# The table of relative biases: 128 copies written to DRAM and read back reversed, in place of matmuls that reverse it

## The reference, cut to what matters

```python
def block(args):
    i, qi = args
    qpos = i * Q_BLOCK + jnp.arange(Q_BLOCK)      # Q_BLOCK = 128
    rel = qpos[:, None] - kpos[None, :]
    bias = bias_table[t5_bucket(rel)].transpose(2, 0, 1).astype(jnp.float32)
    logits = jnp.einsum('bhmqd,bhmkd->bhmqk', qi, kt).astype(jnp.float32) * scale
    logits = logits + bias[None, :, None]
    logits = jnp.where(rel >= 0, logits, -1e30)
```

## Time and profile before

| | us |
|---|---|
| median of three runs | 2764.8 (2764.6 to 2765.83) |
| the profiled execution | 2764.3 |
| its span, first to last instruction | 2762.5 |
| TensorE busy | 2686.8 |
| DVE busy | 1798.8 |
| ACT busy | 1323.2 |
| GpSimd busy | 247.5 |

### The profile page before, as it was taken

How to read it: one execution, slowest core, us unless ns; L and a number is a source line. 1 busy time by engine, 2 the same in 40 slices (tenths; PEclk the granted TensorE clock), 3 DMA queues, 4 the chain that set the end, 5 groups by cost and what they waited for, 6 DMA issues and landing times.

```text
span 2762.5 us, 47112 instructions
## 1 busy us (share of the span) xinstructions
PE 2686.8 (97%) x18110; PEld 2474.7 (90%) x18110; DVE 1798.8 (65%) x2093; ACT 1323.2 (48%) x1603; POOL 247.5 (9%) x181
## 2 busy tenths in 40 slices
PE   8999999999999999999999999799799999999997
PEld 8999899889999888888888889799788888889996
DVE  6676456555545677777764467996677777775444
ACT  4543364464434555555543344544355555554332
POOL 4001200001101100000001231601200000000100
PEclk9999999999999999999999999899899999999998
DMA  7545455545435565555555555355355566555552
GB/s 244 187 157 183 139 182 168 168 165 192 163 122 171 175 189 189 189 189 187 188 189 184 189 185 179 115 177 182 117 179 185 189 189 189 189 189 183 179 186 103
DMA packets 189152, 485.28 MB, mean 176 GB/s; under 512 B 15021, under 2 KB 15029, under 8 KB 188752
## 3 DMA queue, kind: packets, MB, share of 16 engines
q1 hardware_dynamic: 187216, 474.02, 52.8%
q0 software_dynamic: 1792, 9.17, 0.9%
HBM read 481.02 MB, written 2.11 MB: 175 GB/s over the span
## 4 chain that ended last, share of the span: by engine, by line
PE 91%; DVE 6%; ACT 1%; issue 1%; DMA 0%; SPq 0%; ACTq 0%; POOL 0%; DVEq 0%
PE ps L1736 91%; DVE w_lo L1075 2%; DVE op L1121 1%; DVE acc L1550 1%; ACT w_hi L661 1%; DVE hbuf L1706 1%; DVE x_res L1709 0%; DMA raw<-in_weights 0%; ACT op L696 0%; SPq L508 0%; ACT hbuf L1048 0%; ACT yres L1040 0%; ACT L686 0%; DVE mq L1093 0%; DVE rstd L1105 0%
## 5 line engine op out<-in xcount | busy, mean ns | idle before, releaser
L1736 PE MATMUL ps<-op,w_hi 128*128 128x256 f32 (+1 forms) x7232 | 1699.4, 329 | 48.0 <-DVE op L1121 28.5
L1075 DVE TENSOR_TENSOR w_lo<-raw,w_hi 128x1024 fp32r<-128x1024 f32 x900 | 1124.7, 1253 | 866.0 <-ACT w_hi L661 865.1
L661 ACT ACTIVATE w_hi<-raw 128x1024 fp32r<-128x1024 f32 x900 | 950.3, 1059 | 1165.1 <-PE ps L1736 1148.7
L1736 PE MATMUL ps<-op,w_lo 128*128 128x256 f32 x5024 | 1182.8, 281 | 0.0
L1736 PEld LDWEIGHTS ps<-op,w_hi 128*128 128x128 f32 x7232 | 1126.5, 192 | 55.0 <-issue 32.8
L1736 PEld LDWEIGHTS ps<-op,w_lo 128*128 128x128 f32 x5024 | 957.9, 191 | 125.8
L1736 PE MATMUL ps<-g,w_hi 128*128 128x256 f32 (+1 forms) x2112 | 474.8, 319 | 0.0
L1736 PE MATMUL ps<-g,w_lo 128*128 128x256 f32 x1408 | 340.0, 282 | 0.0
L1736 PEld LDWEIGHTS ps<-g,w_hi 128*128 128x128 f32 x2112 | 326.1, 188 | 0.0
L1736 PEld LDWEIGHTS ps<-g,w_lo 128*128 128x128 f32 x1408 | 264.3, 188 | 32.4
L1736 PE MATMUL ps<-w_hi,op 128*128 128x512 f32 x512 | 163.5, 394 | 0.0
(11 more groups left out here) (257 smaller groups left out, 1534.1 us busy)
## 6 DMA issues: line engine op xcount, KB each, us to landing
raw<-in_weights SPq DMA_DIRECT2D x900, 512.0 KB, 4.2
x_res<-in_x SPq DMA_DIRECT2D x8, 256.0 KB, 7.6
mem_x<-in_mem POOLq DMA_DIRECT2D x1, 2048.0 KB, 8.6
x_res<-in_x POOLq DMA_DIRECT2D x1, 2048.0 KB, 9.8
out_x<-x_res POOLq DMA_DIRECT2D x8, 256.0 KB, 2.3
rel_rev<-rel_dram POOLq DMA_DIRECT2D x1, 1024.0 KB, 6.0
hg_con<-in_hg_consts POOLq DMA_DIRECT2D x1, 576.0 KB, 7.4
par<-in_params POOLq DMA_DIRECT2D x1, 538.0 KB, 7.0
```

What stands on the lines that cost most here:

```text
L661: nc.scalar.activation(w_hi[:, s], raw[:, s], ACT.Copy).then_inc(hi_rounded, 1)
L1075: TT(w_lo[:, s], raw[:, s], w_hi[:, s].bitcast(F32), ALU.subtract).then_inc(chunk_split, 1)
L1736: return nc.tensor.matmul(out, lhsT, rhs, start=start, stop=stop, skip_group_check=True)
```

## The change

The rows are written to DRAM 128 times instead of once: `rel_dram` grows to 128 x 8 x 384, and the source repeats `rel_row` with a step of zero. The load then reads, for partition p, copy p from element 127 - p on (a step of one copy less one element), and writes into `bias` itself. The reversal matmuls, their matrix `flip` and its load, ACT's four copies and the waits between them go. TensorE waits for `std_ready` before block 1 instead of at chunk 14, and DVE waits for `rel_loaded` before its first softmax.

```diff
-            pool.dma_start(flip[:, :], A["flip"]).then_inc(table_loaded, 16)
@@ x_and_table, GpSimd
                 if j == 4:
                     pool.wait_ge(rel_copied, 1)
-                    pool.dma_start(rel_dram, rel_row[:, :]).then_inc(rel_stored, 16)
+                    pool.dma_start(rel_dram.rearrange("p h n -> h p n"), spread(rel_row[:, :], P)).then_inc(rel_stored, 16)
                 if j == 6:
                     pool.wait_ge(rel_stored, 16)
-                    shifted = bass.AP(rel_dram.tensor, 0, [[1, P], [NREL, HEADS], [1, TOK]])
-                    pool.dma_start(rel_rev[:, :, :], shifted).then_inc(rel_loaded, 16)
+                    shifted = bass.AP(rel_dram.tensor, P - 1, [[HEADS * NREL - 1, P], [NREL, HEADS], [1, TOK]])
+                    pool.dma_start(bias[:, :, :], shifted).then_inc(rel_loaded, 16)
@@ ACT
-            def bias_out():
-
-                for j in range(4):
-                    act.wait_ge(bias_flipped, j + 1)
-                    nc.scalar.activation(bias[:, 2 * j:2 * j + 2], results(1, j), ACT.Copy).then_inc(bias_made, 1)
-
@@ softmax_top, DVE
                 if item == 0:
-                    dve.wait_ge(bias_made, 4)
+                    dve.wait_ge(rel_loaded, 16)
@@ beside_first, TensorE
                 if (b, c) == (0, 5):
-                    pe.wait_ge(table_loaded, 48)
+                    pe.wait_ge(table_loaded, 32)
                     mm(ps[0:HEADS, 4, 0:NREL], relb[0:33, :], onehot[:, :], True, True).then_inc(rel_sum, 1)
                 if (b, c) == (0, 12):
                     pe.wait_ge(consts_loaded, 32)
                     sums(0, True)
-                if (b, c) == (0, 14):
-                    pe.wait_ge(rel_loaded, 16)
+                if (b, c) == (1, 0):
                     pe.wait_ge(std_ready, STD_END[0])
-                    for h in range(HEADS):
-                        last = mm(ps[:, 4 + h // 2, (h % 2) * TOK:(h % 2 + 1) * TOK], flip[:, :], rel_rev[:, h], True, True)
-                        if h % 2:
-                            last.then_inc(bias_flipped, 1)
-                if (b, c) == (1, 0):
-                    pe.wait_ge(bias_made, 4)
```

More of the change, by code:

```diff
@@ L258, in build @@
         bias = slab("bias", 80)
-        rel_rev = slab("rel_rev", 40)
         rel_row = inside("rel_row", [HEADS, NREL], 72 * KB)
         onehot = inside("onehot", [33, NREL], 74 * KB)
-        flip = inside("flip", [P, P], 77 * KB)
         lam_in = inside("lam_in", [P, 4, 64], 76 * KB)
@@ L308, in build @@
         ps = ctx.enter_context(nc.psum_tensor("ps", [P, 8, BANK], F32))
-        rel_dram = nc.dram_tensor("rel_dram", [HEADS, NREL], F32, kind="Internal").ap()
+        rel_dram = nc.dram_tensor("rel_dram", [P, HEADS, NREL], F32, kind="Internal").ap()
         def pc(name, i=0, n=1):
@@ L333, in build @@
         dve_steps, act_steps = sem("dve_steps"), sem("act_steps")
-        rel_sum, rel_copied, bias_flipped, bias_made = (sem(n) for n in ("rel_sum", "rel_copied", "bias_flipped", "bias_made"))
+        rel_sum, rel_copied = sem("rel_sum"), sem("rel_copied")
         lam_summed, lam_exped, lb_shifted, lb_exped = (sem(n) for n in ("lam_summed", "lam_exped", "lb_shifted", "lb_exped"))
@@ L745, in _ @@
             run_product(act, GM["hg_fm"], split, nothing, both(by_slot(in_pair, SLOTS, range(2, 8)), at_slot(11, exponents),
-                                                               at_slot(15, in_root), at_slot(17, bias_out)), also=beside_f)
+                                                               at_slot(15, in_root)), also=beside_f)
             def level_exps(level):
```

## The result

| | median, us | runs | against before (95% interval) |
|---|---|---|---|
| before | 2765.3 | 4 | |
| after | 2795.6 (2792.1 to 2797.1) | 4 | 1.0104 (1.0092 to 1.0117) |

The account below looks back on a forecast made before the run. TensorE, busy 97% of the span, was taken as the bound. Later sums +25.2, removed matmuls -3.3 and lower clock +2.3 gave +24.2 us on 2764.3, 2788.5, stated as 2789 us; range 2770 to 2800 us.

Parts of the forecast that it names:

- What bounds the kernel, and the place to watch: TensorE, 97% busy; at chunk 12 its sumsq matmuls wait for GpSimd's last sum, ready just 0.07 us before.
- What goes: Reversal matmuls on TensorE's path: -3.26 us; ACT's copies, the load of flip and the moved waits: nothing.
- The store: GpSimd's wait for rel_stored: 8 source partitions set the rate, 31 us plus 2.7, landing at 67.8 us; chance 0.64.
- The fixed part: Part of the store's issue-to-landing time that comes on top of the transfer: 2.9 - 0.2 = 2.7 us.
- The eight-engine rival: Store on eight engines at their own speed: 13.6 + 2.7 = 16.3 us, time 2771 to 2772; chance 0.15.
- GpSimd's tail: After the store lands, GpSimd issues the load and sums two pairs: 5.9 us, sums ready at 73.7 us.
- The clock: After TensorE's idle time before the sumsq matmuls, 4.64 us at half speed: +2.3 us.
- The larger transfer also crosses the weight loads: nothing: At 34 to 45 us only two or three weight loads in flight, TensorE stands before needing later ones: no cost.
- the quick store: At GpSimd's wait: store over 16 engines lands after 9.5 us, time 2762 to 2764.5; chance 0.18.

Follow-up runs that it names:

- the kernel without copies: Changed kernel, but its store writes one 12 KB copy and the load steps by one element, leaving the reversal out: 2761.2 us, ratio 0.9986.
- step 4: Changed kernel with the store's eight source rows on partitions 0, 4, ... 28 instead of 0 to 7: 2775.2 us in one run.
- the kernel with the late load: Changed kernel with the load of bias, and the wait for the store before it, moved behind the load of hg_con: 2775.2 us, ratio 1.0036.

## Why the prediction was right, point by point

*What bounds the kernel, and the place to watch*: right. The sums before chunk 12 had no cover, and the shift appears there.

*What goes*: right. -3.26 us were forecast, -4.3 measured with 3.3 in its interval. ACT's copies, the load of flip and the moved waits cost nothing that shows: in the kernel without copies the first matmul behind the reversal moved by 3.27 us, the matmuls' own time.

*The store*: the branch was right (the 8 partitions set the rate), and the total was 2 us short: 33.7 us forecast, 35.74 measured. The 31 us for the transfer were within 1 us: its packets ran for 32. The fixed part was the term too small: 2.7 us taken, 3.6 measured, since the first packet started 3.3 us after the issue, against 1.3 us for the old store (34.06 to 35.34).

That the 31 us came out so close was partly luck. They rest on the 0.21 us over which the old store's eight packets started. The same 12 KB store has its eight starts spread over 0.68 us in the kernel without copies (36.40 to 37.08 us) and over 0.93 in the version with copies made in DRAM (35.58 to 36.50). By the prediction's own working the first would have made 128 x 0.68 = 87 us. The old store shows a row at 0.1 us, the new one at 0.25 (0.74 for a packet of three), so eight packets had not shown the limit that the long store met.

The eight-engine rival's 13.6 us (0.106 us a row on eight engines) was not a bound either; its 0.106 us also counts the queue's 11 tiny packets, without which a row took 0.095. At step 4 a row took 0.06 us (0.18 for three), and 0.06 x 128 would be 8 us, an estimate from the packets of that window.

*GpSimd's tail*: 5.9 us forecast from the landing to the last sum, 6.3 measured (70.1 to 76.35); the 0.5 us from the landing to the issue of the load were not in the forecast. The store's issue began 0.3 us later than before. With the store's 2 us the sums came at +27.9 instead of +25.2.

*The clock*: +2.3 forecast, +3.8 measured. This term was taken from a pause of 4.72 us, after which half clock lasted 4.6 us; after the 29.6 us here it lasted 8.0 us. The two places were not alike, so the row was a poor price for this one.

Together: 27.9 - 3.3 + 3.8 = 28.4 us, against the forecast 24.2; the rest up to 31.2 arises later at a lower clock, 1.5 in the memory attention and 1.3 at 2011 us. No term of the prediction stood for it. The total was 7 us short, and the range held it.

*"The larger transfer also crosses the weight loads: nothing"*: right for this kernel, and wrong as a reason. The loads were slowed from 3.4 to 23.1 us; the prediction counted how many are in flight and not how slow each gets. It cost nothing only since TensorE stood for something else. The step would have misled anyone who had gone on to move the wait: the kernel with the late load keeps 14 us of the loss.

*The rivals*: the quick store is what the version with copies made in DRAM reaches in effect.

## What to carry to other kernels

Before a transfer is made larger, ask which partitions its SBUF side touches: eight neighbours gave 49 GB/s here, eight rows four partitions apart 133. A small form of the transfer is a weak guide to the rate: the starts of its eight packets were spread over 0.21, 0.68 and 0.93 us in three kernels. A broadcast out of a few neighbouring partitions repeats the slow side, and was better made from DRAM. Count it not only for those who wait for it but for every load that shares the DMA engines, and look at the stock of the engine behind those loads. A transfer needed 300 us later belongs behind the work that the queue's engine owes to others.

## What the runs showed of the hardware

The same 1.57 MB from SBUF to DRAM in 1024 rows of 1536 bytes took 35.7 us from partitions 0 to 7, 19.5 from 0, 8, ... 56, and 16.0 from 0, 4, ... 28; from DRAM to DRAM it took 12.9.

Less expected: the slow transfer also held up transfers that don't touch its source. Loads of 512 KB from DRAM into all 128 partitions, on another queue, took 23 us beside the slowest store, 10.6 beside the middle one, 4.5 to 6.6 beside the fastest, and 3.4 without. The Trainium skill, "DMA: Bandwidth & Descriptors", section "Issuing engines are not separate DMA queues", says that DMAs from all issuing engines run on the same 16 DMA engines and interleave there. That fits. The traces also tell where the weights wait. A weight packet was hardly slower beside the slow store: 23.2% of 16 engines over 32 us for 637 packets is 0.19 us each, and before it was 0.17 (53.8% over 30 us for 1477). So the weight packets are not held up while they move, as the store's own are; they start late. Meanwhile the slow store's packets kept 7.4 of the 16 engines busy, and from 41 to 46 us a third of all engine time was idle (100 - 46.4 - 18.5%). That the late weight packets are those behind the store's on these engines is the likely reading, but the traces don't name the engine of a packet.
